# A gated decoder layer in float32: 17 of 44 steps of the w_down product taken to Strassen's scheme

## The reference, cut to what matters

```python
h = rms_norm(x, ffn_norm_g)
u = causal_depthwise_conv(h @ w_up, conv_w, conv_b)
gate, val = jnp.split(u, 2, axis=-1)
x = x + (jax.nn.silu(gate) * val) @ w_down     # 256 x 5632 @ 5632 x 2048
```

## Time and profile before

| | us |
|---|---|
| median of 3 runs | 1466.71 |
| the profiled execution's own time | 1466.32 |
| its span, first to last instruction | 1464.3 |
| PE busy in it | 1455.5 (99%) |
| DVE busy | 932.5 (64%) |
| ACT busy | 768.0 (52%) |
| POOL busy | 431.1 (29%) |

### The profile page before, as it was taken

One profiled execution on the slowest core, in us unless ns is written; L12 is line 12 of the kernel. 1 busy time (PEld: TensorE's weight loads), 2 busy tenths in 40 slices (PEclk: granted clock), 3 DMA queues, 4 the chain that ended last, 5 costly groups with the idle time before them and its releaser, 6 DMA issues.

```text
span 1464.3 us, 24546 instructions
## 1 busy us (share of the span) xinstructions
PE 1455.5 (99%) x7688; PEld 1246.4 (85%) x7688; DVE 932.5 (64%) x1205; ACT 768.0 (52%) x1063; POOL 431.1 (29%) x486
## 2 busy tenths in 40 slices
PE   8999999999999999999999999999999999999999
PEld 6888888888888888888888888888888888888887
DVE  6545455876655557765567778777777777545443
ACT  6544445576766766655454554454554555333332
POOL 1100000323222223550015555655555655000000
PEclk9999999999999999999999999999999999999999
DMA  7666665655555555575566666666666666655554
GB/s 243 194 181 186 186 180 165 193 179 177 158 167 158 158 169 176 186 246 186 186 186 177 198 188 186 185 187 194 193 188 192 179 191 198 201 194 191 190 197 147
DMA packets 130489, 272.09 MB, mean 186 GB/s; under 512 B 10784, under 2 KB 10816, under 8 KB 130192
## 3 DMA queue, kind: packets, MB, share of 16 engines
q1 hardware_dynamic: 129664, 269.12, 59.8%
q0 software_dynamic: 464, 2.42, 0.5%
q10 hardware_dynamic: 320, 0.01, 0.0%
HBM read 269.42 MB, written 2.10 MB: 185 GB/s over the span
## 4 chain that ended last, share of the span: by engine, by line
PE 99%; DVE 0%; DMA 0%; ACT 0%; issue 0%; POOL 0%; DVEq 0%; ACTq 0%; POOLq 0%
PE bank L1346 98%; PE bank L1395 0%; DMA rows_in<-in_attn_norm_g 0%; PE bank L1529 0%; DVE y L1103 0%; PE bank L1569 0%; DVE hT L765 0%; PE bank L1489 0%; ACT hi L417 0%; ACT hT L434 0%; POOL rows_in L1123 0%; DVE lo L740 0%; PE bank L1446 0%; PE bank L1419 0%; PE bank L1476 0%
## 5 line engine op out<-in xcount | busy, mean ns | idle before, releaser
L740 DVE TENSOR_TENSOR lo<-raw,hi 128x1024 fp32r<-128x1024 f32 (+1 forms) x508 | 651.0, 1285 | 425.0 <-ACT hi L417 424.2
L417 ACT ACTIVATE hi<-raw 128x1024 fp32r<-128x1024 f32 (+1 forms) x508 | 535.3, 1055 | 540.9 <-PE bank L1346 536.5
L1346 PE MATMUL bank<-h2T,hi 128*128 128x512 f32 x1408 | 482.8, 394 | 0.0
L1346 PE MATMUL bank<-h2T,lo 128*128 128x256 f32 x1408 | 376.4, 277 | 0.0
L1346 PEld LDWEIGHTS bank<-h2T,hi 128*128 128x128 f32 x1408 | 257.9, 188 | 53.4
L1346 PE MATMUL bank<-hT,hi 128*128 128x512 f32 (+1 forms) x784 | 274.4, 395 | 0.7 <-DVE lo L740 0.7
L1346 PEld LDWEIGHTS bank<-h2T,lo 128*128 128x128 f32 x1408 | 264.4, 188 | 7.8
L1346 PE MATMUL bank<-hi,ffT 128*128 128x512 f32 x704 | 216.8, 389 | 0.4 <-DVE y L1103 0.4
L1346 PE MATMUL bank<-hT,lo 128*128 128x256 f32 (+1 forms) x784 | 215.1, 284 | 0.0
L1346 PE MATMUL bank<-hi,hT 128*128 128x512 f32 x640 | 198.0, 390 | 0.0
L1310 POOL TENSOR_TENSOR u<-u,rms_row 128x256 f32<-128x256 f32 x88 | 121.3, 1378 | 237.9 <-DVE u L1041 220.6
(11 more groups left out here) (198 smaller groups left out, 1224.9 us busy)
## 6 DMA issues: line engine op xcount, KB each, us to landing
raw<-in_w_in SPq DMA_DIRECT2D x176, 512.0 KB, 3.6
raw<-in_w_up SPq DMA_DIRECT2D x176, 512.0 KB, 3.8
raw<-in_w_down SPq DMA_DIRECT2D x88, 512.0 KB, 3.4
raw<-in_w_branch SPq DMA_DIRECT2D x32, 512.0 KB, 3.7
raw<-in_w_out SPq DMA_DIRECT2D x32, 512.0 KB, 3.6
y<-in_x SPq DMA_DIRECT2D x4, 512.0 KB, 7.0
y<-in_x POOLq DMA_DIRECT2D x1, 2048.0 KB, 9.5
out<-y SPq DMA_DIRECT2D x8, 256.0 KB, 3.1
```

The lines of the kernel that those rows point to most:

```text
L417: act.activation(hi[s][:, 0:width], raw[s][:, 0:width], ACT.Copy)\
L740: dve.tensor_tensor(lo[s][:, 0:width], raw[s][:, 0:width], hi[s][:, 0:width].bitcast(f32), ALU.subtract)\
L1346: return pe.matmul(o, l, r, start=start, stop=stop, skip_group_check=True)
```

## The change

The `w_down` product is cut into 44 steps, 22 in each half m of the columns; a step is a pair of row blocks (2k, 2k+1). A plain step works as before: two chunks of 12 matmuls. 17 steps, 7 in the first half and 10 in the second, are done in Strassen's scheme (Winograd's form): the pair is a 2 x 2 block product, tokens t by the two row blocks times row blocks by the two groups of 512 columns, and it takes 7 block products where there were 8. With three passes each that is 21 matmuls instead of 24.

Such a summed step needs sums of the four weight blocks and of the four activation blocks:

- Weights: four DVE adds of 128x512 (`sums13`, `sums24`) into `sum13` and `sum24`. The step has four chunks, where a plain one has two: the first weight block alone (512 wide), the second raw pair, `sum13`, `sum24`. Each goes through ACT's copy to hi and DVE's subtraction to lo and holds one of the four slots. PE's matmuls of the four chunks are 3, 6, 6 and 6.
- Activations ("left"): the pairs 6 to 12 and 0 to 2 get sums in six batches of one or two pairs. `left_sums(b)` is five DVE instructions, `left_hi_part(b)` two ACT copies that wait for the fifth (`left4_raw`), and `left_lo_part(b)` two DVE subtractions.
- Results: four banks hold direct results and four hold partial ones (A and B, which change roles between the halves); DVE adds them up in `add_p1`, `add_v5`, `make_u2_u3`, `add_u2_u3` and `add_direct`, 12 instructions of 128x512 a half where there were 4. ACT copies one bank per half.
- Loads: from the 13th weight block on there are six raw slots. The first use of the two new ones waits on SP until all of `ffT` is done.

The order of the steps: m = 0: six plain ones (0 to 5), then summed and plain in turn (6 to 19), two plain. m = 1: plain (22), then summed and plain in turn (23 to 42), plain (43). In `BATCHES` the third number is the step behind which `left_sums` and `left_hi_part` stand.

The core of the diff:

```diff
+    BATCHES = [(6, 2, 3), (8, 2, 7), (10, 2, 11), (12, 1, 15), (0, 2, 26), (2, 1, 30)]
+    SUMMED = [k + j for k, n, _ in BATCHES for j in range(n)]
+    Step = namedtuple("Step", "m pair made chunk raw")
+    def down_steps():
+        first = [(0, k, None) for k in range(6)]
+        rest = [k for k in range(13, PAIRS)]
+        for i in range(7):
+            first += [(0, SUMMED[i], i), (0, rest[i], None)]
+        first += [(0, k, None) for k in rest[7:]]
+        rest = [k for k in range(PAIRS) if k not in SUMMED]
+        second = [(1, rest[0], None)]
+        for i in range(10):
+            second += [(1, SUMMED[i], i), (1, rest[i + 1], None)]
+        second += [(1, rest[11], None)]
+        table, chunk = [], C_DOWN
+        for i, (m, pair, made) in enumerate(first + second):
+            table.append(Step(m, pair, made, chunk, 2 * i))
+            chunk += 2 if made is None else 4
...
+            for i, step in enumerate(STEPS):
+                for k in range(2):
+                    q = step.raw + k
+                    old = RAW_BEFORE[q]
+                    if old is None and q < SLOTS:
+                        wait_alone(sp, lo_done, C_DOWN + q - AHEAD)
+                    elif old is None:
+                        wait_alone(sp, ffT_done, FT)
+                    else:
+                        was = STEPS[old // 2]
+                        wait_alone(sp, lo_done, was.chunk + old % 2 + 1)
+                        if was.made is not None:
+                            wait_alone(sp, (sum13_done, sum4_done)[old % 2], S_COUNT[was] + 1)
...
+            def down_hi(c, src, width=2 * GRP):
+                act.wait_ge(w_used, c - SLOTS + 1)
+                act.activation(hi[c % SLOTS][:, 0:width], src[:, 0:width], ACT.Copy)\
+                    .then_inc(hi_done, 1)
+                up_step(NU, c - C_DOWN - AHEAD)
...
+            def left_hi_part(b):
+                k, n, _ = BATCHES[b]
+                act.wait_ge(left4_raw, b + 1)
+                if k < 6:
+                    act.wait_ge(w_used, STEPS[k + n - 1].chunk + 2)
+                act.activation(ff_pairs(k, n)[:, :, 0, 0, P:S], left_raw[b][:, :, 0, :], ACT.Copy)                    .then_inc(left_hi, 1)
+                act.activation(leftb[b][:, :, :, 0, :], left_raw[b][:, :, 1:4, :], ACT.Copy)                    .then_inc(left_hi, 1)
+            def down_plain(step):
+                for k in range(2):
+                    if step.chunk + k >= C_DOWN + AHEAD:
+                        down_hi(step.chunk + k, weights_in(step.raw + k))
+            def down_summed(step):
+                down_hi(step.chunk, weights_in(step.raw), GRP)
+                down_hi(step.chunk + 1, weights_in(step.raw + 1))
+                act.wait_ge(sum13_done, S_COUNT[step] + 1)
+                down_hi(step.chunk + 2, sum13)
+                act.wait_ge(sum2_done, S_COUNT[step] + 1)
+                act.wait_ge(sum4_done, S_COUNT[step] + 1)
+                down_hi(step.chunk + 3, sum24)
...
+            for i, step in enumerate(STEPS):
+                if step.made is None:
+                    down_plain(step)
+                else:
+                    down_summed(step)
+                for b, (_, _, at_step) in enumerate(BATCHES):
+                    if i == at_step:
+                        left_hi_part(b)
...
+            def sums13(step):
+                for q in (step.raw, step.raw + 1):
+                    dve.wait_ge(w_landed[RAW_SLOT[q]], 16 * RAW_TURN[q])
+                if S_COUNT[step]:
+                    dve.wait_ge(lo_done, S_LIST[S_COUNT[step] - 1].chunk + 3)
+                b1, b2 = weights(step.raw), weights(step.raw + 1)
+                dve.tensor_tensor(sum13[:, 0:GRP], b1[:, 0:GRP], b1[:, GRP:2 * GRP], ALU.add)
+                dve.tensor_tensor(sum13[:, GRP:2 * GRP], b1[:, GRP:2 * GRP], b2[:, GRP:2 * GRP],
+                                  ALU.add).then_inc(sum13_done, 1)
+            def sums24(step):
+                n, b2 = S_COUNT[step] + 1, weights(step.raw + 1)
+                dve.wait_ge(sum13_done, n)
+                if n > 1:
+                    dve.wait_ge(lo_done, S_LIST[n - 2].chunk + 4)
+                else:
+                    dve.wait_ge(left_done, 2)
+                dve.tensor_tensor(sum24[:, 0:GRP], sum13[:, 0:GRP], b2[:, GRP:2 * GRP], ALU.add)\
+                    .then_inc(sum2_done, 1)
+                dve.wait_ge(sum2_done, n)
+                dve.tensor_tensor(sum24[:, GRP:2 * GRP], sum24[:, 0:GRP], b2[:, 0:GRP], ALU.add)\
+                    .then_inc(sum4_done, 1)
+            def left_sums(b):
+                k, n, _ = BATCHES[b]
+                f, d = whole[b], left_raw[b]
+                a = ff_pairs(k, n).bitcast(f32)
...
+                dve.tensor_tensor(f[:, :, :, :], a[:, :, :, 0, :], a[:, :, :, 1, :], ALU.add)                    .then_inc(whole_done, 1)
+                dve.wait_ge(whole_done, b + 1)
+                dve.tensor_tensor(d[:, :, 0, :], f[:, :, 0, P:S], f[:, :, 1, P:S], ALU.subtract)                    .then_inc(left1_raw, 1)
+                dve.tensor_tensor(d[:, :, 2, :], f[:, :, 0, 0:P], f[:, :, 0, P:S], ALU.subtract)                    .then_inc(left3_raw, 1)
+                dve.wait_ge(left1_raw, b + 1)
+                dve.tensor_tensor(d[:, :, 1, :], d[:, :, 0, :], f[:, :, 0, 0:P], ALU.subtract)                    .then_inc(left2_raw, 1)
+                dve.wait_ge(left2_raw, b + 1)
+                dve.tensor_tensor(d[:, :, 3, :], d[:, :, 1, :], f[:, :, 1, 0:P], ALU.add)                    .then_inc(left4_raw, 1)
+            def left_lo_part(b):
+                k, n, _ = BATCHES[b]
+                dve.wait_ge(left_hi, 2 * b + 2)
+                dve.tensor_tensor(ff_pairs(k, n)[:, :, 0, 1, P:S], left_raw[b][:, :, 0, :],
+                                  ff_pairs(k, n)[:, :, 0, 0, P:S].bitcast(f32), ALU.subtract)                    .then_inc(left_done, 1)
+                dve.tensor_tensor(leftb[b][:, :, :, 1, :], left_raw[b][:, :, 1:4, :],
+                                  leftb[b][:, :, :, 0, :].bitcast(f32), ALU.subtract)                    .then_inc(left_done, 1)
...
+            def down_plain(step, after):
+                for k in range(2):
+                    if step.chunk + k >= C_DOWN + AHEAD:
+                        down_lo(step.chunk + k, weights(step.raw + k))
+                    if after is not None:
+                        (sums13, sums24)[k](after)
+            def down_summed(step):
+                down_lo(step.chunk, weights(step.raw), GRP)
+                down_lo(step.chunk + 1, weights(step.raw + 1))
+                down_lo(step.chunk + 2, sum13)
+                down_lo(step.chunk + 3, sum24)
+            for i, step in enumerate(STEPS):
+                if step.made is None:
+                    after = STEPS[i + 1] if i + 1 < len(STEPS) else None
+                    down_plain(step, after if after is not None and after.made is not None
+                               else None)
+                else:
+                    down_summed(step)
+                for b, (_, _, at_step) in enumerate(BATCHES):
+                    if i == at_step:
+                        left_sums(b)
+                    if i == at_step + (1 if b == 0 else 2):
+                        left_lo_part(b)
+                if i == 20:
+                    add_p1(0)
+                    add_v5(0)
+                    make_u2_u3(0)
+                if i == PAIRS:
+                    add_direct(0)
+                if i == PAIRS + 2:
+                    add_u2_u3(0)
+            add_p1(1)
+            add_v5(1)
+            make_u2_u3(1)
+            add_u2_u3(1)
+            add_direct(1)
...
+            def down_summed(step):
+                m, c, k, end = step.m, step.chunk, step.pair, step is S_LAST[step.m]
+                near, far = DIRECT[m], PARTIAL[m]
+                batch = [b for b in range(len(BATCHES)) if FIRST_OF[b] <= step.made][-1]
+                at_ = step.made - FIRST_OF[batch]
+                s2, s3, s4 = [(leftb[batch][:, at_, j, 0, :], leftb[batch][:, at_, j, 1, :])
+                              for j in range(3)]
+                pe.wait_ge(lo_done, c + 1)
+                down_product(m, far[0], c, 0, *ff_part(2 * k, 0), end).then_inc(w_used, 1)
+                pe.wait_ge(lo_done, c + 2)
+                down_product(m, near[0], c + 1, 0, *ff_part(2 * k + 1, 0))
+                pe.wait_ge(left_done, 2 * batch + 2)
+                down_product(m, near[1], c + 1, 1, *s4).then_inc(w_used, 1)
+                pe.wait_ge(lo_done, c + 3)
+                down_product(m, far[1], c + 2, 0, *ff_part(2 * k, 1), end)
+                down_product(m, far[3], c + 2, 1, *s3, end).then_inc(w_used, 1)
+                pe.wait_ge(lo_done, c + 4)
+                down_product(m, far[2], c + 3, 0, *s2, end)
+                down_product(m, near[2], c + 3, 1, *ff_part(2 * k + 1, 1)).then_inc(w_used, 1)
+            for i, step in enumerate(STEPS):
```

(81 more changed lines are left out.)

132 lines of the change are left out of this document (97 added, 35 removed).

## The result

| | before | changed |
|---|---|---|
| median of the runs, us | 1466.61 (4 runs, 1466.50 to 1466.74) | 1478.73 (4 runs, 1478.55 to 1478.80) |
| span of the profiled execution, us | 1464.3 | 1476.6 |
| mean granted clock of PE | 0.999 | 0.997 |

The changed kernel is slower: ratio 1.0082, 95% interval 1.0065 to 1.0100, which is 12.1 us. The forecast was 1471.2, with a range of 1467.5 to 1476.

A forecast was written before the change was run, and what follows sets the result against it. PE's matmuls, busy 99% of the span, were taken as the bound. Terms: -12.1 + 3 x 3.2 + 2 x 1.7 + 3.2 + 0.4 = +4.5 on 1466.3, plus 0.4 for the median: 1471.2 us, range 1467.5 to 1476.

The forecast's parts named there:

- the stop: PE's halt between the two halves of the w_down product, 0.5 us, claimed to go with the change.
- A turn without a batch: One summed and one plain step with no activation sums: DVE 8.85 of PE's 10.2 us, claimed to cost nothing.
- The two-pair batch: Activation sums behind steps 7, 11, 26: PE pauses of 2.4 and 0.8, 3.2 us each, bounds 2.2 and 4.9.
- The one-pair batch: Activation sums behind steps 15 and 30: PE pauses of 0.9 and 0.8, 1.7 us each, bounds 0.8 and 3.
- Rival 1: Batches hidden behind PE's work if the fifth sum lands by 7.65 of the turn: faster, 1456.6 us; chance 0.13.
- a rival of its own: Clock rival: PE's clock falls behind three long pauses, 1.5 us lost each, giving 1475.7 us; chance 0.07.
- the start: Batch 0 beside POOL, late first steps and late new raw slots: 3.2 us together, bounds 0 and 7.
- the plain price of batch 1: The 3.2 us put on any two-pair batch, here behind step 7, before the start's lateness is added.
- the quiet price: DVE's start-to-start time with POOL silent: 0.33 us for 256 columns.
- the adds of results: DVE's adding up of result banks, placed in plain steps or idle time: 0.4 us late into batch 4.
- the upper bound of 15.9: The whole sum's change in us with all terms at their upper bounds; with all lower ones it was -3.9.
- rival 2: Even: same stalls at their cheap end, start near nothing, 7 to 14.5 us in all: 1464 to 1469; chance 0.22.

The follow-up runs named there:

- The filled pauses: Changed kernel plus 28 matmuls with a zero left operand, 10 behind step 7 and 9 each behind steps 11 and 26: 1475.56 us, ratio 1.0064.
- the later edits of order and of pieces: On top of moved ACT copies: later raw slots and batch 0's copies (1464.04 us), DVE batches in pieces (1460.38), slots from the 17th block (1458.96).

## Why the prediction was wrong

**What was right.** The direction, and the mechanism. 51 matmuls and the stop were to save 12.1; the kernel without batches saved 11.8. A turn without a batch was to cost nothing, and costs nothing. The two-pair batch was to cost 3.2 us at ACT's place in the order: step 27 has 2.42 + 0.51 and two restarts, 3.5 us. The one-pair batch was to cost 1.7: 0.76 + 0.51 + 0.54 = 1.8. Rival 1 asked that the fifth sum land by 7.65 of the turn. Moving ACT's copies took that condition away, and gave 13.7 us, of which the clock is some 4.5.

**The step that failed: the sum has no term for the clock.** It stood as a rival of its own, with a chance of 0.07, three falls and a price of 1.5 us a fall, and set against the forecast, though it is what the forecast's own pauses bring about: it belonged in the sum. The price was right. In the changed kernel the clock was at 0.50 three times, 3.4 us each, of which PE worked 2.9 to 3.1, at half its speed: 1.4 to 1.6 us a fall, 4.5 in all. The filled pauses show the cause: with them the clock did not fall. The Trainium skill's "TensorE: Matmul & The Clock Gate", in its section "Why this matters for your kernels", warns of long idle gaps between bursts of matmuls, and by it I looked for a fall at batch 1 alone. Measured, the clock fell behind the shorter pauses at steps 12 and 27 as well (2.25, and 2.42 with 0.51), and the measurement decides.

**The term that was mis-sized: the start.** I put 3.2 us over the plain price of batch 1. Measured: three pauses of 0.69, 0.78 and 1.20 with restarts, 3.5; step 7's, 1.7; and batch 1 at 3.46 + 0.51 + 0.54 = 4.5 against 3.2. Together 6.5. DVE in order of time shows where, POOL being at work beside it:

```profile
1236.02 1.75 DVE L1278 TENSOR_TENSOR whole<-ffT 128x1024 f32<-128x1024 f32 x1
1237.81 0.74 DVE L1280 TENSOR_TENSOR left_raw<-whole 128x256 f32<-128x256 f32 x1
...
1247.10 1.39 DVE L1293 TENSOR_TENSOR leftb<-left_raw,leftb 128x768 fp32r<-128x768 f32 x1
...
1257.58 0.42 DVE L1195 TENSOR_TENSOR ffT<-conv,ffT 128x256 fp32r<-128x256 f32 x1
...
1263.86 0.69 DVE L1249 TENSOR_TENSOR sum<-raw 128x512 f32<-128x512 f32 x1 [2.46 <-issue]
```

From start to start the first small sum of 256 columns took 0.66 where I had 0.33, the next 0.76, and the 768-wide subtraction 1.32 where I had 0.87. The last block of `ffT` was done at 1258.0 and not at 1255.9, and the loads that wait for it landed so that DVE went on at 1263.9 and not at 1260.9. I had the price of a small instruction beside POOL, 0.76, from the row at 1235.11, but used it only as an upper bound for the later batches and took the quiet price here, though POOL is busy in half of that window. That POOL is what slows DVE is read from such rows; no run took POOL's work away.

**The sum again.** Between its first and last matmul on ffT the changed kernel takes 1472.8 - 1220.9 = 251.9 us for 1004 spacings of 0.2267, 227.6: 24.3 us lost. The pauses are 15.8 + 13 x 0.27 = 19.3 and the clock 4.5, which leaves 0.5. The kernel without batches, with no pause in the product, is over by the same 0.5 (228.1 against 227.6), so that rest most likely does not come from the batches. Forecast was 16.6. The difference of 7.7 is 4.5 of clock, 3.3 of the start and this 0.5, less 0.6 by which the other batches and the adds of results came out cheaper.

**Slips that changed nothing.** Half the way to the upper bound of 15.9 is 1476.9, not 1476, and 7 to 14.5 us of stalls (rival 2) are 1461.6 to 1469.1, not 1464 to 1469; the measured 1478.73 is outside either way. The 0.14 us from a DVE result to PE's matmul holds for the add at 1340.19; behind a subtraction it is 0.05 (1272.08 + 0.69 to 1272.82).

## What to carry to other kernels

Work that is added to an engine with idle time is free only if its place in every in-order queue it passes is free too: ask for each instruction that waits what stands behind it on its own engine. Here ACT, busy for half of the time, cost 13.7 us by two small copies a batch that stood one step too early. A pause of PE of two microseconds can be dearer than its length, so the price of a fall of the clock belongs in the sum as soon as the sum has such pauses. And a stall can be removed without doing less: of the 24.0 us that the batches cost, moving what waits took away 13.7, and the later edits of order and of pieces 6.1 more.
